# A two-block model forward pass on one core: the places of the large buffers in SBUF are moved to multiples of 2 KB

## The reference

```python
def first_block(x, c, ada_w, ...):
    mod = (silu(c) @ ada_w + ada_b).reshape(bsz, DEPTH, 2, 3, D_MODEL)
    for i in range(DEPTH):
        h = rmsnorm(x, norm_g[i, 0]) * (1.0 + scale) + shift
        y = short_conv_mixer(h, ...) if i % 2 == 0 else ssd_mixer(h, ...)
        x = x + gate * rmsnorm(y, norm_g[i, 1])
        h = rmsnorm(x, norm_g[i, 2]) * (1.0 + scale) + shift
        x = x + gate * rmsnorm(swiglu_ffn(h, f_w_in[i], f_w_out[i]), norm_g[i, 3])

def second_block(x, ...):
    proj = rmsnorm(x, norm_mix) @ w_in
    merged = sigmoid(g_a) * (y_a @ w_up_a) + sigmoid(g_b) * (y_b @ w_up_b)
    x = x + merged @ w_out
    u, g = split(causal_dwconv(rmsnorm(x, norm_ffn) @ w_ffn_in, conv_w, conv_b))
    return rmsnorm(x + (silu(g) * u) @ w_ffn_out, norm_final)
```

## Time and profile before

| | us |
|---|---|
| three runs | 2255.58, 2261.09, 2267.8 |
| median of them | 2261.09 |
| the profiled execution | 2257.73 |
| its span, first to last instruction | 2255.9 |

### The profile page before, as it was taken

The page is one execution under the profiler, slowest core; times in us unless marked ns, Lnnn a source line. Parts: engine busy times, 40 slices in busy tenths (PEclk is TensorE's granted clock), DMA queues, the critical chain, the costliest instruction groups (busy, mean ns, idle before and its releaser), DMA issues.

```text
span 2255.9 us, 28975 instructions
## 1 busy us (share of the span) xinstructions
PE 2185.6 (97%) x10440; PEld 1758.1 (78%) x10440; DVE 1229.8 (55%) x1722; ACT 993.5 (44%) x1420; POOL 975.6 (43%) x421
## 2 busy tenths in 40 slices
PE   6999999999999999989999999999999899999998
PEld 4788888888877777767788888878677688888886
DVE  5776765521277777787522221250778755666412
ACT  4324543334445546544534333453555644444332
POOL 3444444346634324334544446556211143444563
PEclk8999999999999999999999999999999999999999
DMA  7553475553315334333233323334221032332232
GB/s 310 211 206 126 153 275 202 184 151 93 116 50 196 126 122 154 113 111 94 66 102 93 93 75 98 115 101 151 95 69 48 29 106 81 103 101 93 77 93 73
DMA packets 74193, 273.88 MB, mean 121 GB/s; under 512 B 8615, under 2 KB 11303, under 8 KB 67832
## 3 DMA queue, kind: packets, MB, share of 16 engines
q1 hardware_dynamic: 70728, 266.77, 36.3%
q10 hardware_dynamic: 3376, 5.90, 0.8%
HBM read 269.24 MB, written 8.12 MB: 123 GB/s over the span
## 4 chain that ended last, share of the span: by engine, by line
PE 76%; issue 14%; POOL 5%; DVE 3%; ACT 1%; DMA 0%; ACTq 0%; POOLq 0%; SPq 0%; DVEq 0%
PE bank L545 60%; POOL wlo L506 5%; PE bank L921 4%; PE bank L568 2%; PE bank L1014 2%; PE bank L978 1%; PE bank L942 1%; PE bank L572 1%; PE bank L961 1%; PE bank L656 1%; PE bank L617 1%; PE bank L609 1%; PE bank L862 1%; DVE x L1561 0%; DMA x<-x_d 0%
## 5 line engine op out<-in xcount | busy, mean ns | idle before, releaser
L506 POOL TENSOR_TENSOR wlo<-raw,whi 128x1024 fp32r<-128x1024 f32 x382 | 930.2, 2442 | 1195.7 <-ACT whi L1052 1195.6
L1052 ACT ACTIVATE whi<-raw 128x1024 fp32r<-128x1024 f32 x382 | 400.9, 1055 | 580.4 <-PE bank L545 549.8
L545 PE MATMUL bank<-h_hi,whi 128*128 128x512 f32 x1616 | 639.7, 396 | 5.1 <-DVE tb L1660 3.3
L545 PE MATMUL bank<-h_hi,wlo 128*128 128x512 f32 x1616 | 634.2, 392 | 0.0
L545 PE MATMUL bank<-h_lo,whi 128*128 128x512 f32 x1616 | 632.5, 391 | 0.0
L545 PEld LDWEIGHTS bank<-h_hi,whi 128*128 128x128 f32 x1616 | 304.0, 188 | 75.2 <-issue 9.7
L545 PEld LDWEIGHTS bank<-h_hi,wlo 128*128 128x128 f32 x1616 | 303.8, 188 | 66.8
L545 PEld LDWEIGHTS bank<-h_lo,whi 128*128 128x128 f32 x1616 | 304.0, 188 | 65.0
L545 PE MATMUL bank<-g_lo,whi 128*128 128x512 f32 x592 | 232.2, 392 | 0.0
L545 PE MATMUL bank<-g_hi,wlo 128*128 128x512 f32 x592 | 232.1, 392 | 0.0
L545 PE MATMUL bank<-g_hi,whi 128*128 128x512 f32 x592 | 230.9, 390 | 0.0
(11 more groups left out here) (343 smaller groups left out, 2930.9 us busy)
## 6 DMA issues: line engine op xcount, KB each, us to landing
raw<-f_in_d SPq DMA_DIRECT2D x88, 512.0 KB, 3.6
raw<-m_d SPq DMA_DIRECT2D x65, 512.0 KB, 3.7
ada_f<-ada_d SPq DMA_DIRECT2D x24, 1024.0 KB, 6.5
raw<-g_in_d SPq DMA_DIRECT2D x44, 512.0 KB, 3.5
raw<-w_in_d SPq DMA_DIRECT2D x41, 512.0 KB, 3.6
csb<-cs_d SPq DMA_DIRECT2D x32, 640.0 KB, 6.5
ada_a<-ada_d SPq DMA_DIRECT2D x16, 1024.0 KB, 4.9
raw<-a_in_d SPq DMA_DIRECT2D x24, 512.0 KB, 5.9
```

Source lines behind the costliest of these rows:

```text
L506: nc.gpsimd.tensor_tensor(wlo[:, s], raw[:, s], whi[:, s].bitcast(F32), ALU.subtract).then_inc(lo_ready, 1)
L545: mm = nc.tensor.matmul(psum[bank][:], w[:, s, kk, :], xs[part == "lo"][:, k, :], start=first and kk == 0 and i == 0, stop=last and kk == ...
L1052: nc.scalar.activation(whi[:, s], raw[:, s], ACT.Copy).then_inc(hi_ready, 1)
```

## The change

The order in which buffers are allocated changes, and nothing else. `vec`, `kst`, `mod` and `csil` come first, then a gap that fills up to the next multiple of `ROW` = 4 x 512 = 2048 bytes, then the ring (`raw`, `whi`, `wlo`), `x` and the working tiles, whose sizes are all multiples of 2048 bytes. So these, and the arena behind them, begin at multiples of 2048 bytes. The arena is now reserved as a tensor of 120 KB, and `ones`, `ncol`, `zcol`, `epscol`, `dtp`, `root` and `ssum` are allocated behind it.

```diff
--- before.py
+++ after.py
@@ -130,27 +130,22 @@
             return ctx.enter_context(nc.sbuf_tensor(name, shape, dt))
 
 
+        vec = sb("vec", [P, NV])
+        kst = sb("kst", [P, NK])
+        mod = sb("mod", [P, 96])
+        csil = sb("csil", [P, KD])
+        ROW = 4 * S
+        sb("gap", [P, -nc.sbuf_base % ROW // 32 * 8])
         raw = sb("raw", [P, RING, CH, P])
         whi = sb("whi", [P, RING, CH, P], F32R)
         wlo = sb("wlo", [P, RING, CH, P], F32R)
         x = sb("x", [P, KD, S])
-        vec = sb("vec", [P, NV])
-        kst = sb("kst", [P, NK])
-        ones = sb("ones", [P, P])
-        mod = sb("mod", [P, 96])
-        csil = sb("csil", [P, KD])
-        ncol = sb("ncol", [P, 4, 2, KD])
-        zcol = sb("zcol", [P, 1])
-        epscol = sb("epscol", [P, 1])
-        dtp = sb("dtp", [P, 2, HEADS])
         acc = sb("acc", [P, S])
         modacc = sb("modacc", [P, S])
         sq = sb("sq", [P, 2, S])
         rstd = sb("rstd", [P, S])
         ta = sb("ta", [P, 2, S])
         tb = sb("tb", [P, 2, S])
-        root = sb("root", [P, 7, NT])
-        ssum = sb("ssum", [P, NT])
         ident = kst[:, K0["ident"]:K0["ident"] + P]
         tri = kst[:, K0["tri"]:K0["tri"] + P]
         qvalid = kst[:, K0["qvalid"]:K0["qvalid"] + NT]
@@ -226,6 +221,15 @@
         tbl = view(G + 78 * KB, "tbl", [BUCKETS + 1, 16])
         mg_hi = view(G + 32 * KB, "mg_hi", [P, KD, S], F32R)
         mg_lo = view(G + 48 * KB, "mg_lo", [P, KD, S], F32R)
+
+        sb("arena", [P, 120 * KB // 4])
+        ones = sb("ones", [P, P])
+        ncol = sb("ncol", [P, 4, 2, KD])
+        zcol = sb("zcol", [P, 1])
+        epscol = sb("epscol", [P, 1])
+        dtp = sb("dtp", [P, 2, HEADS])
+        root = sb("root", [P, 7, NT])
+        ssum = sb("ssum", [P, NT])
 
         banks = ctx.enter_context(nc.psum_tensor("bank", [P, 8, S], F32))
         psum = [banks[:, b, :] for b in range(8)]
```

## The result

| | us | to the kernel before |
|---|---|---|
| before, median of 6 runs (2255.58 to 2267.8) | 2260.86 | |
| after, median of 6 runs (2241.22 to 2249.82) | 2243.87 | 0.9926, interval 0.9913 to 0.994 |

The account below looks back on a forecast made before the run. TensorE's matmul stream was taken as the bound, 8256 matmuls at 229 ns, 1891 of 2255.9 us. Four terms of 0 left the time unchanged: 2259 us, midway between profiled run and timed median; range 2246 to 2274.

Parts of the forecast that it names:

- step 4: DMAs, ring loads and kernel start: new landing addresses cost 0, bound 0.7 us either way on the 12 us before first work.
- Step 1: TensorE's matmul stream: boundary crossings and operands' relative phase don't matter; cost 0, at most 7 ns either way per reacting matmul.
- Rival A: Matmul stream gets faster as moving rows start aligned: up to 15.6 ns each, 2130 us; at 7 ns, 2201; chance 0.08.
- Rival B: Weight loop: every fourth weight tile newly shares its moving row's phase and collides; 7 ns on 2064 matmuls, 2273 us; chance 0.06.
- Step 2: VectorE: whether two inputs share a phase doesn't matter; cost 0, bound 0.3 us.
- Step 3: ScalarE's copy and GpSimd's split: their buffers keep one common phase, so nothing changes; 100 ns more per split would stay hidden.

## Why the prediction was wrong

*The frame was right.* The pace of 8256 large matmuls decides the kernel, and the test named for the prediction, the pace of the piece of 1536 within 1.4 ns of 228.9, is the one that failed: it moved by 2.2. Priced with the runs, the 8256 less the 1026 of the state-space stage are 7230; 7230 x 2.2 = 15.9 us, with the 1.1 us at the start 17.0, the difference of the medians. That it fits to 0.1 us is luck: the interval of the ratio, 0.9913 to 0.994, is some 14 to 20 us, the 1.1 us may not be the change's (step 4), and the 2.2 ns are those of the long piece. In the chain's pieces of 72 the gain is 1.5 ns a matmul, (16.60 - 16.49)/72, here before and after:

```profile
117.51 16.60 PE bank L545 x72
```
```profile
115.45 16.49 PE bank L549 x72
```

For distance 32 against 0 the same working gives 7230 x 6.65 = 48.1, and 2292.25 - 2243.87 is 48.4 (two sets of runs, ratios 1.0139 and 0.9926). The profiled executions differ by less, 14.4 us, and some goes back where stages meet: by the starts of the same matmuls the lead falls from 7.1 us at 626 us to 6.0 at 690, and from 11.8 at 1690 to 10.1 at 1786.

*Step 1 failed, in its last part.* "Whether moving and stationary operands have the same phase doesn't matter either" rested on 274 ns for cg with bg and a median of 273 for csb with xdt. These are durations, so latencies, of small products between other work. The cost is in the distance between starts in an unbroken stream: the runs' paces go from 226.7 to 234.3 while a weight load stays at 188 or 189 ns. The large products of the trace before all stood at one distance, 64 within 256, so the trace couldn't bear that sentence, and the chance of 0.8 for no change was too high for it. In the sum this is the term put at 0: the runs give it 15.9 us by the pace, and the profiled executions 13.3, their 14.4 less 1.1 at the start. The bound of 7 ns a matmul held for this change (2.2); at the worst distance the cost is 7.6. The other part of step 1 was right: crossing a boundary of 2048 bytes costs nothing, with everything at 128 or at 0 it is 348.21.

*Rival A* had the direction and a wrong cause: the start of the row by itself. The arena alone at 0 is 1.06% slower. Its lower price, 7 ns, was three times too large. Of the 15.6 ns that it asked about, the distance explains 2.2; 13.4 are still there at the best one. The Trainium skill, TensorE: Matmul & The Clock Gate, section Back-to-back issue gap, has 216 ns for the isolated gap of one matmul of 512 columns, and about 131 for one in a stream of pairs of weight load and matmul. The best stream here has 226.7, longer than both, and the measurement decides.

*Rival B* named the right two operands, weight tile and moving row, and had the sign wrong: equal places are the best case, not a collision. That it is the next tile's load that meets the row is not shown; the kernel with whi alone moved speaks against it as a rule. Its price of 7 ns is about that of most unequal places.

*Step 2* held: the minima on VectorE are 691 again. *Step 3*: the split takes 2431 ns, 11 less than in the earlier trace rows, and nothing came of it. But the step left out what a split does to VectorE beside it. The share of 5% for line 506 in the earlier trace rows already showed that some stage's chain runs by way of the splits, and there the faster matmuls bring 0.5 us.

*Step 4*: ring loads land in 3.5 to 3.6 us at 0, and in 3.5 to 3.7 at 128 (before, and in the kernel with raw, x and the working tiles at 128), so the 6% estimated for a start off a multiple of 256 bytes is not to be seen. But the start moved by more than its bound of 0.7 us:

```profile
13.81 0.75 DVE L1623 TENSOR_SCALAR bank<-ada_first,csil 128x512 f32<-128x512 f32 x1 [12.75 <-DMA ada_first<-ada_d]
```

That is 1.14 us before the 14.95 of the earlier trace rows. It doesn't follow from the places of raw and x: with both at 0 the same instruction starts at 13.81 (after) and 15.49 us (ring alone at 0), with both at 128 at 13.98 and 15.13. Over all kernels the profiled executions have 13.64 to 15.47 where the distance is 0 within 256 and 14.14 to 16.22 where it isn't. The two ranges overlap and each is wider than 1.14 us, so with one profiled execution of each kernel the earlier start can't be put down to the change.

## What to carry to other kernels

In a stream of float32r matmuls of 512 columns that load a new weight tile each time (other types and shapes weren't measured), the distance between stationary and moving operand within 256 bytes is worth up to 3.4% of the pace (226.7 to 234.3 ns): put both on the same place within 256, and never let the sizes of small constants decide it, since one half of an alignment can be worse than none. A claim that something doesn't matter needs the quantity on which the kernel depends, here the time from start to start in the stream, and a case in the trace where the cause varies. Count a gain per instruction only over the stretches whose chain consists of that instruction.

## What was not expected of the hardware

The paces come in steps. At distance 0 three starts are 680.0 ns apart; at 64 the intervals 226, 229 and 232 repeat (686.7); at 192 they are 231 and 236 by turns (466.7, 13.3 more than two of 226.7); at 128 seven intervals repeat (228, 230, 232, 241, 232, 231, 232, 40 ns more than seven), and both kernels with that distance have the same seven. All these excesses are multiples of 6.67 ns, 16 cycles at 2.4 GHz. The rhythm pays no heed to which of the three products an interval belongs to, and with whi at another distance than wlo, one program changes between rhythms. What unit behind the reads has this grain, no run shows.
